# Two norms inside a two-block transformer kernel, worked in halves of the tokens

## What is computed

```python
x = x + rmsnorm(merged @ w_out[l], norm_mix_post[l])     # norm "post1"
h = rmsnorm(x, norm_mlp_pre[l])                          # norm "n2"
f = jnp.square(jax.nn.relu(h @ w_ff_in[l])) @ w_ff_out[l]
x = x + rmsnorm(f, norm_mlp_post[l])                     # norm "post2"
...
xn = rmsnorm_2(x, norm_mix_g[l])                         # norm "n3"
proj = xn @ w_in[l]
```

## Time and profile before

| | us |
| --- | --- |
| median of 3 runs | 1455.29 |
| lowest and highest | 1452.25, 1455.32 |
| the profiled execution's own time | 1453.19 |
| its span, first to last instruction | 1451.4 |
| TensorE busy | 1412.6 |
| VectorE busy | 885.8 |
| ScalarE busy | 612.7 |

### The profile page before, as it was taken

The page is one execution under the profiler, slowest core; times in us unless marked ns, Lnnn a source line. Parts: engine busy times, 40 slices in busy tenths (PEclk is TensorE's granted clock), DMA queues, the critical chain, the costliest instruction groups (busy, mean ns, idle before and its releaser), DMA issues.

```text
span 1451.4 us, 17505 instructions
## 1 busy us (share of the span) xinstructions
PE 1412.6 (97%) x7116; PEld 1139.0 (78%) x7116; DVE 885.8 (61%) x1305; ACT 612.7 (42%) x977; POOL 1.9 (0%) x7
## 2 busy tenths in 40 slices
PE   6999999999999999999998999999999999999997
PEld 5777777787788888887786777778878888888886
DVE  6987764757635355354767888579964443453446
ACT  5453553423312222132425777788553321331232
POOL 0000000000000000000000000000000000000000
PEclk9999999999999999999999999999999999999999
DMA  4222214231323323333131121323233333333223
GB/s 166 88 83 93 59 59 145 73 108 57 116 88 101 102 88 102 90 99 108 38 116 55 48 59 58 102 73 101 88 100 91 101 102 89 100 97 106 88 87 102
DMA packets 37583, 131.60 MB, mean 91 GB/s; under 512 B 4432, under 2 KB 6608, under 8 KB 37248
## 3 DMA queue, kind: packets, MB, share of 16 engines
q1 hardware_dynamic: 37152, 127.16, 28.9%
q0 software_dynamic: 352, 3.34, 0.6%
HBM read 128.39 MB, written 2.10 MB: 90 GB/s over the span
## 4 chain that ended last, share of the span: by engine, by line
PE 83%; DVE 9%; ACT 5%; issue 2%; DMA 1%; SPq 0%; DVEq 0%; ACTq 0%
PE gp L1556 23%; PE gp L1557 23%; PE gp L1558 23%; PE mp L1749 2%; PE mp L1760 2%; PE mp L1730 2%; ACT w_hi L475 2%; DVE w_lo L897 2%; PE mp L1633 1%; PE mp L1635 1%; PE mp L1634 1%; PE mp L1704 1%; PE mp L1675 1%; PE mp L1710 1%; PE mp L1649 0%
## 5 line engine op out<-in xcount | busy, mean ns | idle before, releaser
L1556 PE MATMUL gp<-h_hi,w_hi 128*128 128x512 f32 x944 | 370.0, 392 | 3.7 <-DVE h_lo L941 1.9
L1558 PE MATMUL gp<-h_hi,w_lo 128*128 128x512 f32 x944 | 367.5, 389 | 0.0
L1557 PE MATMUL gp<-h_lo,w_hi 128*128 128x512 f32 x944 | 367.5, 389 | 0.0
L897 DVE TENSOR_TENSOR w_lo<-raw,w_hi 128x1024 fp32r<-128x1024 f32 x202 | 246.4, 1222 | 136.4 <-ACT w_hi L475 135.9
L1556 PE MATMUL gp<-a_hi,w_hi 128*128 128x512 f32 x692 | 271.9, 393 | 1.7 <-DVE w_lo L897 1.6
L1557 PE MATMUL gp<-a_lo,w_hi 128*128 128x512 f32 x692 | 269.4, 389 | 0.0
L1558 PE MATMUL gp<-a_hi,w_lo 128*128 128x512 f32 x692 | 269.4, 389 | 0.0
L475 ACT ACTIVATE w_hi<-raw 128x1024 fp32r<-128x1024 f32 x202 | 211.3, 1050 | 136.9 <-PE gp L1558 70.5
L1556 PEld LDWEIGHTS gp<-h_hi,w_hi 128*128 128x128 f32 x944 | 177.2, 188 | 45.1 <-issue 4.1
L1558 PEld LDWEIGHTS gp<-h_hi,w_lo 128*128 128x128 f32 x944 | 177.2, 188 | 37.3
L1557 PEld LDWEIGHTS gp<-h_lo,w_hi 128*128 128x128 f32 x944 | 177.3, 188 | 36.0
(11 more groups left out here) (279 smaller groups left out, 1576.7 us busy)
## 6 DMA issues: line engine op xcount, KB each, us to landing
raw<-slabs SPq DMA_DIRECT2D x202, 512.0 KB, 3.6
arena<-slabs SPq DMA_DIRECT2D x30, 512.0 KB, 3.6
arena<-x_in SPq DMA_DIRECT2D x4, 512.0 KB, 6.5
arena<-x_in POOLq DMA_DIRECT2D x1, 2048.0 KB, 8.3
out_t<-arena SPq DMA_DIRECT2D x8, 256.0 KB, 2.2
arena<-bias POOLq DMA_DIRECT2D x1, 1024.0 KB, 5.2
arena<-s5b SPq DMA_DIRECT2D x1, 512.0 KB, 9.4
arena<-s5c SPq DMA_DIRECT2D x1, 512.0 KB, 10.7
```

The lines of the kernel that those rows point to most:

```text
L897: TT(w_lo[:, n % RING, :], raw(n), w_hi[:, n % RING, :].bitcast(F32), ALU.subtract).then_inc(w_lo_ready, 1)
L1556: pe.matmul(dst, hi, x_hi(t), start=t == 0, stop=False)
L1557: pe.matmul(dst, hi, x_lo(t), start=False, stop=False)
L1558: ins = pe.matmul(dst, lo, x_hi(t), start=False, stop=t == tiles - 1)
```

## The change

Both norms are worked in two halves of 256 tokens.

- The last two slabs in front (places 6 and 7, `TAIL` and `TAIL + 1`) are multiplied for the first 256 tokens of both, then for the second 256 tokens of both. Inside the second half of slab 6 stand the sums, and later the spread, of the first half's norm. Both slabs keep their ring places until their second halves are done.
- The first four slabs behind run all chunks for the first half of the tokens, then all for the second. The second half's sums stand after the first two chunks of the first half, its spread after the sixth.
- `keep_clock` is gone.
- `updates` has 16 turns of half width in place of 8. Between turns 1 and 3 stand VectorE's parts for the late halves of slabs 6 and 7, and the splits of the third and fourth slab behind the norm (`split(slab + AHEAD)` and `split(slab + START - 1)`, AHEAD 2 and START 4). Before, the third of these was split in front of the norm. ScalarE has the same order in `turn_of_stage`.
- In front of the second norm, VectorE's half sum of squares stands after the half additions of both slabs; in front of the first, ahead of the scaling of slab 6.
- Squares of the new x have a semaphore of their own (`sq_apart`), the counts of the others are renumbered, and the tail's helpers are renamed and shared.
- POOL's load of the distances waits for `X_AT["post2"]`, now 16 turns.

The core of the diff; the renumbering, the tail's renaming and repeated parts are left out:

```diff
+            def turn_of_stage(kind, nxt, gain, late_square, slab):
+
+                at = X_AT[kind]
+                half_root(kind, 0)
+                normalised(nxt, gain, at, 0, (0, 1))
+                late_square(TAIL)
+                split(slab + AHEAD)
+                normalised(nxt, gain, at, 0, (2,))
+                late_square(TAIL + 1)
+                split(slab + START - 1)
+                normalised(nxt, gain, at, 0, (3,))
+                half_root(kind, 1)
+                normalised(nxt, gain, at, 0, range(4, DC))
+                normalised(nxt, gain, at, 1, range(DC))
+                split(slab + START)
+                root(nxt)
+                split(slab + START + 1)
...
+            def late_ff(m):
+                act.wait_ge(late_half, HALVED["post2"] + m - TAIL + 1)
+                half_square("post2", 1, m, Fo[:, m, tokens(1)])
...
-            def updates(kind, nxt, pre, scale, fourth):
+            def updates(kind, nxt, pre, scale, late, slab):
...
+                def update(n):
+                    i, c = turns[n]
+                    dve.wait_ge(scaled, first + n + 1)
+                    TT(X[:, c, tokens(i)], X[:, c, tokens(i)], tmp[c % 2][:, tokens(i)], ALU.add).then_inc(x_new, 1)
+                    if n + 1 < len(turns):
+                        scaled_by_rms(n + 1)
+                    dve.wait_ge(a_hi_ready, A_AT[nxt] + n + 1)
+                    STT(out=a_lo[:, c, tokens(i)], in0=X[:, c, tokens(i)], scalar=col(pre, c),
+                        in1=a_hi[:, c, tokens(i)].bitcast(F32), op0=ALU.mult, op1=ALU.subtract).then_inc(a_lo_ready, 1)
+
+                half_invert(kind, 0)
                 scaled_by_rms(0)
...
+                update(0)
+                update(1)
+                late(TAIL)
+                split(slab + AHEAD)
+                update(2)
+                half_add_square(kind, 1)
+                late(TAIL + 1)
+                split(slab + START - 1)
+                update(3)
+                half_invert(kind, 1)
+                for n in range(4, len(turns)):
+                    update(n)
                 fold_squares(nxt)
...
+            def last_pair(kind, name, k0, x_hi, x_lo):
+
+                for m in (k0 + TAIL, k0 + TAIL + 1):
+                    pe.wait_ge(w_lo_ready, SLAB[name] + m + 1)
+                    pe.wait_ge(out_read, freed_by(name, m))
+                    half_slab(SLAB[name] + m, half_bank(name, 0, m), x_hi, x_lo, 8, 0).then_inc(early_half, 1)
+                for m in (k0 + TAIL, k0 + TAIL + 1):
+                    then = {0: lambda: half_first_squares(kind, 0), 2: lambda: half_last_square(kind, 0),
+                            6: lambda: half_spread(kind, 0)} if m == k0 + TAIL else {}
+                    half_slab(SLAB[name] + m, half_bank(name, 1, m), x_hi, x_lo, 8, 1, then).then_inc(half_done, 2)
...
+            def start_halves(name, kind, old, then):
+
+                chunks = range(DC)
+                order = [(c, e) for c in (0, 1) for e in range(START - 1)] + [(c, START - 1) for c in (0, 1)]
+                order += [(c, e) for c in chunks[2:] for e in range(START)]
+                late = [(c, e) for c in range(TOGETHER) for e in range(START)]
+                late += [(c, e) for e in range(START) for c in range(TOGETHER, DC)]
...
-            keep_clock("q2", 5)
-            last_square("post2")
-            keep_clock("q2", 2)
-            spread("post2")
-            keep_clock("q2", 10)
```

More of the change, by code:

```diff
@@ L877, in _ @@
                     act.wait_ge(tail_added, 2 * i + m - TAIL + 1)
[L878 to L884, removed]
+                    half_square("n5", i, m, X[:, m, tokens(i)])
+                half_root("n5", i)
         @block.vector
@@ L1256, in updates, with scaled_by_rms @@
[L1256 to L1264, removed]
-                fold_squares(nxt)
-            invert_root("post1", keep=False)
+                turns = [(i, c) for i in range(2) for c in range(DC)]
+                def scaled_by_rms(n):
+                    i, c = turns[n]
+                    if c == 0:
+                        dve.wait_ge(rms_spread, NORM[kind] + i + 1)
+                    if n >= 2:
+                        dve.wait_ge(x_new, first + n - 1)
+                    scale(i, c).then_inc(scaled, 1)
@@ new lines, in updates @@
+                split(slab + START)
+                invert_root(nxt)
+                split(slab + START + 1)
+            for m in (TAIL, TAIL + 1):
+                split(SLAB["out"] + AHEAD + m)
+            for m in (TAIL, TAIL + 1):
+                if m == TAIL:
+                    half_add_square("post1", 0)
+                dve.wait_ge(sq_done, SQ_AT["post1"] + m + 1)
+                dve.wait_ge(early_half, HALVED["post1"] + m - TAIL + 1)
+                TS(Y[:, m, tokens(0)], half_bank("out", 0, m), col("g_mix_post", m), None, ALU.mult).then_inc(out_read, 1)
@@ L1601, in mean_of_folded, with half_first_squares @@
                 ins.then_inc(rms_sum, 1)
-            def keep_clock(name, count):
-                pe.wait_ge(w_lo_ready, SLAB[name] + 1)
-                for _ in range(count):
-                    pe.matmul(mp[:, 4, :], w_hi[:, SLAB[name] % RING, 0:P], h(0), start=True, stop=True)
+            def half_first_squares(kind, i):
+                pe.wait_ge(sq_added, ADDED_AT[kind] + TAIL + i)
+                for b in (2 * i, 2 * i + 1):
+                    pe.matmul(half_norm(i)[:, b:b + 1], ssum[:, b * P:(b + 1) * P], ones[:, 0:1], start=b % 2 == 0, stop=False,
+                              skip_group_check=True)
@@ new lines, in half_slab @@
+            def half_slab(n, dst, x_hi, x_lo, tiles, i, then={}):
+                for t in range(tiles):
+                    cols = slice(t * P, (t + 1) * P)
+                    hi, lo = w_hi[:, n % RING, cols], w_lo[:, n % RING, cols]
+                    pe.matmul(dst, hi, x_hi[:, t, tokens(i)], start=t == 0, stop=False)
+                    pe.matmul(dst, hi, x_lo[:, t, tokens(i)], start=False, stop=False)
+                    ins = pe.matmul(dst, lo, x_hi[:, t, tokens(i)], start=False, stop=t == tiles - 1)
+                    if t in then:
+                        then[t]()
+                return ins
@@ L1793, in _ @@
                      (lambda t: pe.wait_ge(h_lo_ready, H_AT["z2"] + t + 1)) if j == 0 else None)
-            for k in range(DC):
-                a_stage("out", k, a_wait("merged") if k == 0 else None,
-                        then={5: lambda: first_squares("post1")} if k == DC - 1 else {})
-            keep_clock("ff", 1)
-            last_square("post1")
-            keep_clock("ff", 2)
-            spread("post1")
-            keep_clock("ff", 12)
+            for k in range(TAIL):
+                a_stage("out", k, a_wait("merged") if k == 0 else None)
+            last_pair("post1", "out", 0, a_hi, a_lo)
             def ff1_part(p, last=False):
@@ L1890, in tail_slab @@
             def tail_slab(i, m, then={}):
[L1891 to L1893 removed]
+                pe.wait_ge(w_lo_ready, LAST_SLAB + m + 1)
                 if i == 0:
[L1895 to L1903 removed]
```

254 lines of the change are left out of this document (136 added, 118 removed).

## The result

| | us |
| --- | --- |
| median before, these runs | 1455.18 |
| median after, 4 runs | 1473.42 |
| lowest and highest after | 1470.82, 1477.39 |
| ratio and its 95% interval | 1.0133, 1.0103 to 1.0162 |
| the profiled execution after | 1471.48 (span 1469.7) |

A forecast was written before the change was run, and what follows sets the result against it. The prediction read TensorE as busy for 97% of the span, VectorE 61%. Profiled 1453.19 + 8.0 for the schedule + 1.6 for one clock fall = 1462.8, with 1.2 on top: 1464 us, range 1456 to 1469.

The forecast's parts named there:

- The half chunk: On VectorE behind each norm: a half chunk takes 1.41 us, so a whole one 2.82 in place of 2.15.
- the row's 0.52: Price taken for the half copy with a scale on ScalarE, which the trace lacked; its bounds were 0.36 and 0.52.
- The sum of the schedule: Order of work at both norms, step by step: +3.1 us at the first, +4.7 at the second, taken as +8.0.
- The fourth slab's waits: TensorE waits for the fourth slab's split weights: 2.2 us at the first norm, 3.2 at the second.
- The clock's term: The granted clock falls once, at the second norm, without keep_clock: +1.6 us.
- a wait of 1 us for the second spread: At the first norm, VectorE waits about 1 us for the spread that ends at 342.47.
- A: Rival, both norms: TensorE becomes the bound and VectorE's chain hides; 10 us gained, 1443 to 1445; chance 0.06.
- B: Rival, both norms: half instructions cost half, half chunk cycle 1.08 us, sum +0.4, 1454 to 1456; chance 0.10.
- C: Rival on the clock at the norms: no fall, 1462 (chance 0.30); falls at both norms, 1466 (chance 0.22).

The follow-up runs named there:

- the run that fills all but these: The changed kernel plus unread products in its waits, except those ahead of the fourth slab of ff and q2: 1466.4 us.
- the last run: Changed kernel with chunks 4 to 7 whole, third and fourth slab's splits early, sums and spreads moved, mean asked for behind the fourth slab: 1451.6 us, ratio 0.9973.
- all waits filled: The changed kernel plus unread products in its seven waits, at both norms, nothing taken out: 1462.62 us, ratio to before 1.0048.

## Why the prediction was right and where it failed

**The half chunk was right.** Copies, adds and pace behind the second spread, VectorE and ScalarE in order of time:

```profile
347.12 0.42 DVE L1294 TENSOR_TENSOR arena<-arena 128x256 f32<-128x256 f32 x1
...
347.58 0.51 ACT L517 ACTIVATE a_hi<-arena,par 128x256 fp32r<-128x256 f32 x1 [0.58 <-DVE arena L1294]
...
348.52 0.42 DVE L1294 TENSOR_TENSOR arena<-arena 128x256 f32<-128x256 f32 x1
```

1.40 us a half chunk, 1.41 forecast; the copy takes 0.51, and the row's 0.52 was the right end of its bounds. The Trainium skill, VectorE: DVE Perf Modes, section on the TRN2 errata, gives 0.40 as an estimate; the measurement decides against it. Its warning about instructions under 512 elements on SBUF is borne out by the price: two halves take 2.80 us, where a whole chunk took 2.15. (That row has 0.73 us for the whole copy, not the 0.72 of the prediction; nothing hangs on it.)

**The sum of the schedule was right.** +3.1 and +4.7 forecast; 45.20 − 42.24 = +3.0 and 49.19 − 44.62 = +4.6 with the clock kept. The whole kernel then costs 7.2 us, where the sum said 8.0. Each wait came from the engine that was named, within 0.3 us where the clock was up ahead of it (1.75 for 2.0, 1.80 for 2.0, 2.54 for 2.7). The fourth slab's waits were shorter, 0.96 and 1.79 for 2.2 and 3.2, because TensorE came to them late, at half clock; in the run that fills all but these they are 1.96 and 3.03.

**The clock's term failed:** one fall, 1.6 us, where it was 10.8. The mechanism was named and its single price stands (1.4 and 1.5 at the first norm). Three things in the step were wrong. It counted falls by comparison with the longest idle row it had, 2.86 us, and passed over waits of 2 us; 1.76 us was enough, though not every time: waits of 1.80 us here and 1.94 in the last run were followed by no fall. It looked at the waits for weights alone; the waits for the fold and the mean's narrow products behind them cost 3.7 us. And it priced each fall as if wide products followed; with a second wait and the sums close behind, the lower level lasted 10 us at the first norm. Its place was wrong as well: at the first norm it counted none.

**What that low clock moves:** the forecast gave VectorE a wait of 1 us for the second spread. After has it 2.8, and with all waits filled it is 1.09. VectorE in order of time, after:

```profile
344.99 0.42 DVE L1337 TENSOR_TENSOR arena<-arena,mp 128x256 f32<-128x256 f32 x1 [2.80 <-PE mp L1686]
```

This is how a slow TensorE delays a chain that VectorE bounds: what it loses ahead of that spread has no cover.

**The rivals.** A (TensorE as the bound, 1443 to 1445) didn't come true, and for the reason given against it, both splits behind the chunks; the last run, with the splits moved and half of the chunks whole, got 3.3 of its 10 us. B is out by the half chunk's 1.40 us. C was the right rival with too narrow a span: 1466 for falls at both norms. The range left it out by 4 us.

## What to carry to other kernels

Unread products in a wait are part of the schedule: whoever moves the waits has to move them along, and price their loss by what stands behind each wait until the clock is back, not by the wait. Cutting a chunk in two made it dearer on VectorE and ScalarE, 2.80 us in place of 2.15; do it only for as many chunks as the early start needs (the last run does it for four of eight), and put the splits that TensorE waits for ahead of the chunk work.

## What the runs showed of the hardware

- A single wait of 1.76 us between wide products brought the granted clock to 0.50, and not in the wait but in the products behind it; by 335, some 4 us later, it was back. With a wait of 2.54 us in the changed kernel it fell inside the wait, at 702. The Trainium skill, TensorE: Matmul & The Clock Gate, Part 1, says that throttled is the default and activity releases it; these traces agree.
- The length of a wait alone doesn't settle it. Waits of 1.80 and 1.94 us were followed by no fall. The sum of squares of a norm in the second block, which no run here edits, has the same wait of 0.82 us in the traces of the kernel before (ahead of 1083.72) and of the last run (ahead of 1078.54): the granted clock stays at 1.00 in the first and is 0.50 from 1080 to 1084 in the second.
- It also fell with no wait over 0.32 us, half a microsecond behind the last of 16 narrow instructions between wide ones, at one norm and not at the other in the same execution. Cut into two parts of 8 with wide products between, they were followed by no fall in that profile, but neither were the 16 in one piece in the kernel before and in the last run.
- A kernel's times scatter along with the clock: the kernel before without unread products ran from 1453.27 to 1460.35 us, at a mean granted clock of 0.993 in its three shortest executions and of 0.987 to 0.990 in the others.
